# Differential attention and output projection of a hybrid decoder block as one stage instead of two

## The reference, cut to what matters

```python
def diff_mixer(...):                      # 4 heads, two maps m per head, blocks of 128 queries
        sc = einsum('bhmqd,bhmkd->bhmqk', qblk, k) * scale        # causal
        p = softmax(sc)
        a = p[:, :, 0] - lam * p[:, :, 1]
        return einsum('bhqk,bhkv->bhqv', a, v)
    o = rms_norm(o, g_sub) * (1.0 - lambda_init)
...
        h = h + concatenate([o_gla, o_diff], -1) @ w_out[l]       # (1024 x 1024) @ (1024 x 1024)
        h = h + peer_mixer(rms_norm(h, g_ffn[l]), ...)            # the experts
```

## Time and profile before

| | us |
|---|---|
| median of three runs | 3209.05 (3208.2 to 3211.4) |
| the profiled execution, its time | 3208.9 |
| its span in the trace | 3207.2 |
| first softmax unit starts / `diff_attention` ends | 409.6 / 601.6 |
| `project_out` ends (last split on DVE) | 703.5 |

### The profile page before, as it was taken

One profiled execution on the slowest core, in us unless ns is written; L12 is line 12 of the kernel. 1 busy time (PEld: TensorE's weight loads), 2 busy tenths in 40 slices (PEclk: granted clock), 3 DMA queues, 4 the chain that ended last, 5 costly groups with the idle time before them and its releaser, 6 DMA issues. The chain is left out here.

```text
span 3207.2 us, 49336 instructions
## 1 busy us (share of the span) xinstructions
PE 3043.3 (95%) x17450; PEld 1711.2 (53%) x17450; DVE 2321.1 (72%) x4680; ACT 1004.6 (31%) x1471; POOL 1279.3 (40%) x899
## 2 busy tenths in 40 slices
PE   8898889889999699999969999999999999999999
PEld 4444645445555477777635555555555554444444
DVE  3234465438999666666558888888888888999996
ACT  4322255323343355555411222222222222222221
POOL 1021111002443212212156666666655555555662
PEclk9999567899999799999989999999999999999999
DMA  3210010121121244555488888878888888888884
GB/s 106 70 40 0 14 40 1 34 79 55 64 73 52 93 175 186 196 196 185 171 283 287 271 292 280 274 272 289 287 275 274 272 273 287 303 305 292 309 293 174
DMA packets 256174, 594.91 MB, mean 185 GB/s; under 512 B 20768, under 2 KB 127408, under 8 KB 252976
## 3 DMA queue, kind: packets, MB, share of 16 engines
q1 hardware_dynamic: 180016, 318.63, 29.3%
q0 software_dynamic: 73728, 268.47, 23.7%
q10 hardware_dynamic: 2304, 6.29, 0.6%
HBM read 513.63 MB, written 79.69 MB: 185 GB/s over the span
## 5 line engine op out<-in xcount | busy, mean ns | idle before, releaser
L238 PE MATMUL f_y<-f_v_hi,f_a_hi 128*128 128x512 f16 x1536 | 583.5, 380 | 9.5 <-DVE p_h L2212 9.5
L239 PE MATMUL f_y<-f_v_lo,f_a_hi 128*128 128x512 f16 x1536 | 583.3, 380 | 0.0
L240 PE MATMUL f_y<-f_v_hi,f_a_lo 128*128 128x512 f16 x1536 | 583.3, 380 | 0.0
L2179 POOL DMA_INDIRECT f_rows<-in_peer_u,p_row_index x256 | 355.9, 1390 | 207.0 <-DVE f_rows L2220 124.4
L2179 POOL DMA_INDIRECT f_rows<-in_peer_v,p_row_index x256 | 310.9, 1215 | 280.7 <-DVE p_h L2230 252.4
L2220 DVE SCALAR_TENSOR_TENSOR f_rows<-f_rows,p_xs 128x1024 f32<-128x1024 f32 x256 | 379.8, 1517 | 46.5 <-DMA f_rows<-in_peer_u,p_row_index 46.5
L2230 DVE SCALAR_TENSOR_TENSOR p_h<-f_rows,f_row_a,p_h 128x1024 f32<-128x1024 f32 x256 | 394.3, 1540 | 17.6 <-DMA f_rows<-in_peer_v,p_row_index 10.8
L2212 DVE SCALAR_TENSOR_TENSOR p_h<-f_y,p_h 128x512 f32<-128x512 f32 x384 | 262.9, 685 | 109.5 <-PE f_y L240 107.5
L2190 POOL TENSOR_TENSOR f_v_lo<-f_v_in,f_v_hi 128x1024 f16<-128x1024 f32 x128 | 283.6, 2216 | 145.0 <-ACT f_v_hi L2154 143.7
L238 PE MATMUL f_hid<-p_act_hi,x_u_hi 128*128 128x384 f16 x1008 | 330.5, 328 | 2.0 <-DVEq L2197 2.0
L239 PE MATMUL f_hid<-p_act_lo,x_u_hi 128*128 128x384 f16 x1008 | 330.3, 328 | 0.0
(11 more groups left out here) (311 smaller groups left out, 5461.4 us busy)
## 6 DMA issues: line engine op xcount, KB each, us to landing
f_v_in<-in_peer_v SPq DMA_DIRECT2D x128, 512.0 KB, 5.2
dense_weights<-e_stage SPq DMA_DIRECT2D x24, 2048.0 KB, 8.7
f_g_in<-dense_weights SPq DMA_DIRECT2D x32, 1536.0 KB, 15.6
x_u_in<-in_peer_u SPq DMA_DIRECT2D x64, 512.0 KB, 4.9
e_u_in<-in_peer_u SPq DMA_DIRECT2D x48, 512.0 KB, 4.1
x_gel<-early_tiles SPq DMA_DIRECT2D x64, 384.0 KB, 3.4
early_tiles<-e_gel SPq DMA_DIRECT2D x48, 384.0 KB, 2.5
a_w_in<-in_w_in SPq DMA_DIRECT2D x24, 512.0 KB, 3.8
```

The source lines that it names most:

```text
L238: pe.matmul(out, a_hi, b_hi, start=first, stop=False)
L239: pe.matmul(out, a_hi, b_lo, start=False, stop=False)
L240: return pe.matmul(out, a_lo, b_hi, start=False, stop=last)
L2179: nc.gpsimd.indirect_dma_start(out=rows[q % ROWS][:], out_offset=None, in_=table, in_offset=bass.IndirectOffsetOnAxis(ap=T.row_index[:, ti ...
```

## The change

The two stages become one, `diff_project`. The units stay, and the work on a finished token tile t is put between the units of later tiles:

- unit 4t+5 (`TURN_O`): its head outputs are turned and split; unit 4t+6 and 4t+7 (`PROJECT`): the 48 matmuls, in four parts of 12 (two parts a unit, one ahead of `turn_probs`, one ahead of `values`); unit 4t+8 (`ADD`): x is added, the sum squared, and normalised; unit 4t+9 (`TURN_X`): the normed tile is turned and split. Tile 7, and the end of tile 6, follow the last unit.
- PSUM has room for one `acc` only; the turned outputs and the turned normed tile (`o_turn`, `x_turn`) lie in it too. So `a_ps` is halved: for b of 4 and more the probabilities are turned in two goes of at most four blocks (`turn_probs(u, 0)` ahead of `scores(u+1, 1)`, `turn_probs(u, 1)` behind it), and ACT copies out twice. `e`, `a`, `a_t` have one buffer instead of two.
- `w_out` is loaded through two 128x1024 buffers (`T.xs`) and split in units 0 to 3, two row blocks a unit (`w_high` on ACT, `w_low` on DVE). All of x is loaded into `T.h` as soon as the queries and keys, which now lie there, are turned.
- Aliases elsewhere: `project_in` takes `junk` and `w_in` from `T.rows` and `T.xs`; one stage boundary is gone.

```diff
+    TURN_O, PROJECT, ADD, TURN_X = DIFF_H + 1, DIFF_H + 2, 2 * DIFF_H, 2 * DIFF_H + 1
...
 sync
+            for k in range(KT):
+                if k >= 2:
+                    sp.wait_ge(w_lo_done, k - 1)
+                sp.dma_start(w_in[:, k % 2, :], io.w_out[0, k * P:(k + 1) * P, :]).then_inc(w_loaded[k % 2], 16)
+                if k == 1:
+                    sp.dma_start(gain[:], io.g_ffn[0, :].partition_broadcast(P)).then_inc(gain_loaded, 16)
+                    sp.wait_ge(qk_turned, 2 * NT)
+                    for t in range(NT):
+                        sp.dma_start(T.h[:, t, :], io.x[0, t * P:(t + 1) * P, :]).then_inc(x_loaded, 16)
...
 tensor
+            for u in range(LAST):
+                if more:
+                    scores(u + 1, 0)
+                for t in tile_at(u, TURN_X):
+                    turn_normed(t)
+                for n in range(2):
+                    for t in tile_at(u, PROJECT + n):
+                        project(t, 2 * n)
+                if u < NU:
+                    turn_probs(u, 0)
+                if more:
+                    scores(u + 1, 1)
+                if b >= 4:
+                    turn_probs(u, 1)
+                for t in tile_at(u, TURN_O):
+                    turn_output(t)
+                for n in range(2):
+                    for t in tile_at(u, PROJECT + n):
+                        project(t, 2 * n + 1)
+                if u < NU:
+                    values(u)
...
 scalar
+                for t in tile_at(u, TURN_X):
+                    normed_hi(t)
...
+                for t in tile_at(u, ADD):
+                    square_h(t)
+                if u < NU:
...
+                    output(u)
+                for t in tile_at(u, TURN_O):
+                    output_hi(t)
+                if 2 * u < KT:
+                    w_high(2 * u)
+                    w_high(2 * u + 1)
...
 vector
+                if u < NU:
+                    combine(u)
+                for t in tile_at(u, ADD):
+                    add_x(t)
+                for t in tile_at(u, TURN_X):
+                    normed_lo(t)
+                if more:
+                    for m in range(2):
+                        maximum(u + 1, m)
+                if 0 < u <= NU:
+                    norm(u - 1)
+                for t in tile_at(u, ADD):
+                    normalise(t)
+                for t in tile_at(u, TURN_O):
+                    output_lo(t)
+                if 2 * u < KT:
+                    w_low(2 * u)
+                    w_low(2 * u + 1)
```

More of the change, by code:

```diff
@@ L844, in _, with diff_project, tile_at @@
                                                    ALU.subtract).then_inc(lo_done, 1)
-def diff_attention(nc, io, T):
+def diff_project(nc, io, T):
     SCALE = DIFF_DK ** -0.5
     units = [(b, h) for b in range(NT) for h in range(DIFF_H)]
+    NU = len(units)
+    LAST = NU + 6
+    turns = [1 + (b >= 4) for b, _ in units]
+    turns_before = [sum(turns[:u]) for u in range(NU + 1)]
+    def tile_at(u, first):
+        t, off = divmod(u - first, DIFF_H)
+        return [t] if off == 0 and 0 <= t < NT else []
+    TURN_O, PROJECT, ADD, TURN_X = DIFF_H + 1, DIFF_H + 2, 2 * DIFF_H, 2 * DIFF_H + 1
     with ExitStack() as ctx:
@@ L969, in turn, with project @@
                 for h in range(DIFF_H):
-                    last = pe.transpose(turned[:, h, :], o_n[:, b % 2, h, :], T.ident[:])
+                    last = pe.transpose(o_turn[:, h, :], o_n[:, t % 2, h, :], T.ident[:])
                 last.then_inc(o_turned, 1)
+            def project(t, part):
+                if part == 0:
+                    pe.wait_ge(o_lo, t + 1)
+                    if t == 0:
+                        pe.wait_ge(w_lo_done, KT)
+                toks = slice(t * P, (t + 1) * P)
+                for k in (2 * part, 2 * part + 1):
+                    for half in range(2):
+                        cols = slice(half * HALF, (half + 1) * HALF)
+                        last = split_mm(pe, acc[:, cols], T.act_hi[:, k, toks], T.act_lo[:, k, toks],
+                                        w_hi[:, k, cols], w_lo[:, k, cols], k == 0, k == KT - 1)
+                if part == 3:
+                    last.then_inc(acc_done, 1)
@@ L973, in _, with turn_normed @@
+            def turn_normed(t):
+                pe.wait_ge(normed, t + 1)
+                for k in range(KT):
+                    last = pe.transpose(x_turn[:, k, :], normed_tile(t)[:, k * P:(k + 1) * P], T.ident[:])
+                last.then_inc(x_turned, 1)
             for m in range(2):
                 scores(0, m)
-            for u, (b, h) in enumerate(units):
-                more = u + 1 < len(units)
+            for u in range(LAST):
+                b = units[u][0] if u < NU else 0
+                more = u + 1 < NU
@@ L1030, in _, with normed_hi @@
+            def normed_hi(t):
+                act.wait_ge(x_turned, t + 1)
+                nc.scalar.activation(T.act_hi[:, :, t * P:(t + 1) * P], x_turn, ACT.Copy, scale=S_ACT).then_inc(x_hi, 1)
             for m in range(2):
                 exps(0, m)
-            for u, (b, h) in enumerate(units):
-                probs_out(u)
-                if u + 1 < len(units):
-                    for m in range(2):
-                        exps(u + 1, m)
-                output(u)
-                if h == 1 and b:
-                    turned_hi(b - 1)
@@ new lines, in normalise, with normed_lo @@
+            def normalise(t):
+                dve.wait_ge(x_rstd, t + 1)
+                dve.wait_ge(gain_loaded, 16)
+                if t:
+                    dve.wait_ge(x_turned, t)
+                nc.vector.scalar_tensor_tensor(normed_tile(t), T.h[:, t, :], xss[:, t:t + 1], gain[:], ALU.mult,
+                                               ALU.mult).then_inc(normed, 1)
+            def normed_lo(t):
+                dve.wait_ge(x_hi, t + 1)
+                toks = slice(t * P, (t + 1) * P)
+                nc.vector.scalar_tensor_tensor(T.act_lo[:, :, toks], x_turn, S_ACT, T.act_hi[:, :, toks], ALU.mult,
+                                               ALU.subtract).then_inc(x_lo, 1)
@@ L2290, in allocate_constants, with allocate_rows @@
     return T
+def allocate_rows(S, T):
+    T.h = S.sb("h", [P, NT, D])
+    T.xs = S.sb("xs", [P, NS, D])
+    T.rows = S.sb("rows", [P, 2, NS, PICKS])
+    T.row_index = T.rows[:, 0].bitcast(U32)
+    T.row_weight = T.rows[:, 1]
+    T.dq, T.dk = (T.h[:, 4 * n:4 * n + 4, :].rearrange("p t d -> p (t d)").rearrange("p (t n) -> p t n", t=NT)
+                  for n in range(2))
 def allocate_diff(S, T):
```

305 lines of the change are left out of this document (118 added, 187 removed).

## The result

| | us |
|---|---|
| kernel before, median of 4 runs | 3208.62 (3207.76 to 3211.4) |
| changed kernel, median of 4 runs | 3229.77 (3224.85 to 3234.4) |
| ratio, 95% interval | 1.0064 [1.0046, 1.0082] |
| profiled execution, time and span | 3224.85 and 3223.1 |

Slower by 21 us, where 29 were forecast. The profiled execution of the changed kernel was its fastest run, 5 us under the median. Its span is 15.9 us longer than before's, and all of it arises in the new stage: the stage ends at 719.5 (703.5 before, 732.5 forecast), and behind it come 2503.6 us (2503.7 before).

What follows compares the result with a forecast made beforehand. Bound: a unit loop through four engines, with PE slack. Up to unit 31 insertions cost 129.2 us and the faster loop returns 27.5; behind it 72.7 less: +29.0, 3238 us, range 3204 to 3266 (own case 3224 to 3252).

Steps and rivals of the forecast that it cites:

- Splitting w_out: Units 0 to 3: weight splits on ACT and DVE delay the next reciprocal, 3.95 us a unit, 15.8 us.
- N: Unit 4t+8: normalisation on DVE, waiting for square and root, delays the next reciprocal; 3.37 us in six tiles, 20.2 us.
- X: Unit 4t+9: the normed tile's low half on DVE delays the maxima; 1.5 us in six tiles, 9 us.
- O: Unit 4t+9: splitting the next tile's head outputs delays the reciprocal; 2.15 us in seven tiles, 15.1 us.
- A: A tile's first 12 matmuls, ahead of the turning, at half clock; seven times 5.1 less 9.8 covered, 25.9 us.
- Clock in idle units: PE at half clock in 4t+9 lengthens turning, scores and values, delaying the output; about 12 us, bounds 0 and 20.
- The other 36 matmuls: Units 4t+6 to 4t+8: a tile's remaining projection matmuls exceed the loop's room on PE; 22.8 plus 8.4 us.
- The base loop: 27 unit loops from unit 4 to 31 at full clock, with turning in two goes; 136.9 us, before 164.4.
- The tail: From the reciprocal of unit 31 to the stage's end: remaining work of tiles 6 and 7, 41.8 us, before 114.5.
- Rival 1: PE's clock stays full throughout from the first projection; 3202 us, chance 0.16.
- Rival 2: Stalls N, X and O, 44.3 us together, are hidden while PE works off its lag; 3194 us, chance 0.10.
- Rival 3: PE's clock does not rise during a tile's first 12 matmuls, so later work costs more; 3266 us, chance 0.12.

Runs made afterwards that it cites:

- e1: Changed kernel without splitting w_out in units 0 to 3 (constants instead, only two of eight row blocks loaded); +1.6 us over the kernel before, ratio 1.0009.
- e2: Changed kernel with the normalisation taking a constant instead of waiting for GpSimd's root; -0.5 us against the kernel before, ratio 0.9997.
- c0: The changed kernel run once more, unedited, as a control; +19.0 us over the kernel before, ratio 1.0055.
- e6: Changed kernel with 12 extra matmuls on PE in each unit 4t+8, results overwritten; +21.1 us over the kernel before, ratio 1.0067.
- e5: Changed kernel with the three VectorE stalls taken apart by order and place, projection parts half a unit later; -14.4 us against the kernel before, ratio 0.9956.
- e7: Kernel before with only the halved bank, probabilities turned and copied in two goes, and single buffers; -10.6 us against the kernel before, ratio 0.9969.

## Why the prediction was right, and what was mis-sized

The sign held, and so did the main of the mechanism: work and waits in the in-order queues lengthen the unit loop. Measured +21, forecast +29 with 3224 to 3252 as its own range. That it came so near is in part luck, since large errors of both signs cancel. And by the trace, in which the sum was made, the miss is 13 us and not 8: the stage ended at 719.5 where 732.5 was forecast.

- *Splitting w_out*, 15.8: the two traces have 15.5 and 16.0 more in units 0 to 4, and e1 took 17.4 off by the medians. Right; the blocks were hardly late.
- *N*, 20.2: 19.5 by the medians, 16.4 by the traces, of which 12.4 stand in the loop, for which the term was meant. The 3.37 us a tile was exact (3.36); a quarter of what e2 gained in these units is made up for behind them.
- *X*, 9: 8 to 10 by the medians, 5 to 7 in the loop. Right in size.
- *O*, 15.1: 8 to 10 by the medians, 5 to 7 in the loop. Too large, and this is a step that failed: "2.15 us ahead of the next reciprocal", taken as a loss of the loop. VectorE did wait, even 4.4 us; but PE had its own arrears in that unit, and only its wait of 8.4 us in all counts.
- *A*, 25.9: too large, and here the premise failed. "At half clock ... 12 take 5.1 us" held for tiles 1 and 2 only; for tiles 0, 3, 4, 5 and 6 the matmuls at the start of part 0 followed each other in 0.22 us, the full clock. Two times 5.1 and five times 2.6 less 9.8 is 13.4, so 12.5 too much by the forecast's own formula. In c0 only tile 3 started at the half clock. The price of such a start was right: 2.5 and 2.9 us in units 18 and 10 of the two traces, for 5.1 - 2.6.
- *Clock in idle units*, 12: the half-clock values were there (2.87 us in unit 21), and where they ran faster the unit was shorter: by 1.55 us in unit 9 and 0.79 in unit 13 (e6), by 1.29 in unit 29 (c0). An estimate from these three is 5 to 9 us for the six units. The term was rather too large, and no run measures it alone.
- *The other 36 matmuls*, 31.2: not measured apart. e5 less e7, 198.6 - 149.6, puts the 300 matmuls that lie between these two reciprocals, with their turnings, at 49.0 us, where A, these and the clock were forecast at 69.1. It is their price in the order of e5 and at its clock.
- *The base loop*, 136.9: too low. It took the full clock from unit 4 on, which was to give 27.5 us back. The loop of e7, with no projection in it, takes 149.6 and gives 14.8 back; PE's clock in its first units is not full (0.50 from 427 to 449 us, 0.69 from 445 to 461), and units 4 and 5 take 3.99 and 4.00 us where 3.4 was forecast.
- *The tail*, 41.8: 43.4.

From unit 4 to 31 the forecast had 250.3 us and the trace has 235.0. In parts: base loop 149.6 for 136.9 (+12.7), the projection with A and clock 49.0 for 69.1 (-20.1), the three stalls together 36.4 for 44.3 (-7.9). In this division, one of several, what the clock costs in the stalled units counts with the stalls. So the small miss of 8 us in the end is made of larger ones of both signs. The signs that were named are there: reciprocals of units 0 to 4 seven apart, VectorE waiting for GpSimd and for ScalarE, four units of band 3 in 33.6 us (about 35 forecast); the clock at 0.50 at the start of a tile is not, in five of seven. The prediction named the clock at 1.00 at the start of the tiles as a sign that it is wrong, and for those five this part of it was. Rival 1 (clock full) was right about them, and wrong about the time, 3202. Rival 2 was wrong for the change as made, and describes e5. Rival 3 did not occur.

One thing the argument did not see: the stalls were not the price of merging the stages, only of where three steps stood. With them a unit or half a unit further on the merged stage beats the kernel before, by 14.4 us, and by 30.4 with the weights spread out.

## What to carry to other kernels

When work is put between the steps of a loop, try to place each consumer a whole unit behind its producer, behind and not ahead of what the next round waits for. Price a wait by what the engine that bounds the loop loses, not by the longest wait in the profile: 25.8 us of waiting on VectorE were worth 8 to 10 by the medians and 5 to 7 in the loop. Spread extra work over as many rounds as have slack in its engine: two weight blocks in each of four units cost 15.5 us, one in each of eight 4.9. And run the same program twice before reading a difference of 2 us out of a trace.
